# Writing out the two layers of a decoder step, with fewer blocks that clear semaphores

## What is computed

```python
hp, hs = x_prompt, x_sample
for l in range(DEPTH):                       # DEPTH = 2
    mixer_w = (w_in[l], w_conv[l], lower[l], hg_norm[l], w_out[l])
    tail_w = (w_xq[l], w_xo[l], ln2_g[l], ln2_b[l], w_up[l], w_down[l], ln3_g[l], ln3_b[l])
    y, ... = token_mixer(hp, pos_p, *mixer_w, conv0, hg0, dsa_prompt)
    hp = layer_norm(DN_ALPHA * hp + y, ln1_g[l], ln1_b[l])
    hp = cross_and_ffn(hp, mk, mv, *tail_w)
    ...                                      # the same for hs, with paged caches
```

## Time and profile before

| | us |
|---|---|
| median of 3 runs | 3986.69 (3983.5 to 3986.92) |
| the profiled execution | 3984.36 |
| its span, from its first to its last instruction | 3982.5 |

### The profile page before, as it was taken

The page is one execution under the profiler, slowest core; times in us unless marked ns, Lnnn a source line. Parts: engine busy times, 40 slices in busy tenths (PEclk is TensorE's granted clock), DMA queues, the critical chain, the costliest instruction groups (busy, mean ns, idle before and its releaser), DMA issues. The chain is left out here.

```text
span 3982.5 us, 51084 instructions
## 1 busy us (share of the span) xinstructions
PE 3676.5 (92%) x19290; PEld 2740.2 (69%) x19290; DVE 2117.1 (53%) x4222; ACT 1047.1 (26%) x2166; POOL 1176.6 (30%) x1043
## 2 busy tenths in 40 slices
PE   6999978899888999999989999878899889999998
PEld 4454664467677999999845546644666679999997
DVE  4899665553255333333569995555532553333335
ACT  2301133451232221111432112345412321111123
POOL 3014673323032122111430156723120321112224
PEclk9999956999999999999989999579999999999999
DMA  4111002561212111111121010045412121111111
GB/s 150 44 48 39 11 6 91 173 212 53 74 43 85 42 42 42 42 42 42 39 75 43 29 47 6 1 146 178 152 53 74 43 85 42 42 42 42 42 42 56
DMA packets 143260, 255.17 MB, mean 64 GB/s; under 512 B 24801, under 2 KB 76386, under 8 KB 142818
## 3 DMA queue, kind: packets, MB, share of 16 engines
q1 hardware_dynamic: 130786, 215.00, 15.8%
q0 software_dynamic: 12288, 37.76, 2.7%
HBM read 231.31 MB, written 21.42 MB: 63 GB/s over the span
## 5 line engine op out<-in xcount | busy, mean ns | idle before, releaser
L2601 PE MATMUL ps<-ffn_parts 128*128 128x384 f32 (+1 forms) x4608 | 777.2, 329 | 22.7 <-POOL ffn_parts L2766 22.7
L2601 PEld LDWEIGHTS ps<-ffn_parts 128*128 128x128 f32 x4608 | 773.1, 189 | 25.9 <-POOL ffn_parts L2766 23.7
L2611 PE MATMUL ps<-ffn_parts 128*128 128x512 f32 x3328 | 767.9, 390 | 1.9 <-DVE ffn_parts L2823 1.9
L2611 PEld LDWEIGHTS ps<-ffn_parts 128*128 128x128 f32 x3328 | 621.0, 188 | 140.3 <-DVE arena L2836 11.2
L2836 DVE TENSOR_TENSOR arena<-arena,ps 128x1024 f32<-128x1024 f32 x270 | 329.6, 1221 | 304.2 <-PE ps L2611 300.3
L919 PE MATMUL ps<-arena,arena_w 128*128 128x384 f32 (+1 forms) x1152 | 359.5, 475 | 3.6 <-PEq L454 2.6
L2771 POOL TENSOR_TENSOR ffn_parts<-arena,ffn_parts 128x1024 fp32r<-128x1024 f32 x64 | 154.8, 2418 | 566.2 <-ACT ffn_parts L2687 566.2
L928 PE MATMUL ps<-arena_w,arena 128*128 128x512 f32 (+3 forms) x864 | 318.6, 526 | 2.4 <-ACT mix_rest L1104 2.4
L919 PEld LDWEIGHTS ps<-arena,arena_w 128*128 128x128 f32 x1152 | 221.9, 193 | 141.1 <-issue 11.2
L329 DVE TENSOR_SCALAR_CACHE_REDUCE mix_rest<-mix_rest,small 128x384 bf16<-128x384 f32 (+4 forms) x330 | 278.7, 875 | 2.1
L2816 DVE TENSOR_TENSOR arena<-arena 128x384 f32<-128x384 f32 (+1 forms) x96 | 77.0, 829 | 352.7 <-ACT arena L2691 352.7
(11 more groups left out here) (333 smaller groups left out, 5191.7 us busy)
## 6 DMA issues: line engine op xcount, KB each, us to landing
arena<-in_w_down SPq DMA_DIRECT2D x32, 1024.0 KB, 7.4
arena_w<-in_w_in SPq DMA_DIRECT2D x10, 2048.0 KB, 8.5
arena_w<-in_kv SPq DMA_DIRECT2D x64, 256.0 KB
mix_rest<-in_kv SPq DMA_DIRECT2D x64, 256.0 KB
ffn_raw<-in_w_up SPq DMA_DIRECT2D x16, 1024.0 KB, 5.5
arena<-in_w_up SPq DMA_DIRECT2D x16, 1024.0 KB, 5.5
arena<-out_y_prompt SPq DMA_DIRECT2D x2, 4096.0 KB, 14.5
arena_w<-in_mem_kT SPq DMA_DIRECT2D x16, 512.0 KB, 7.0
```

Source lines behind the costliest of these rows:

```text
L2601: ins = pe.matmul(bank(3 * c + b, y - x), w[:, k, :], h[:, k, x:y], start=(k == 0 and h is HH and w is WH), stop=(k == KC - 1 and w is WL))
L2611: ins = pe.matmul(bank((6, 0)[j % 2] + a), u[:, c, tcol(t)] if t < NT - 1 else u[:, c, :], d[:, c, 512 * a:512 * a + 512], start=(first an ...
```

## The change

The loop over the layers becomes a Python loop, so the body stands in the program twice and `layer` is a constant; tensors and semaphores get names with a number. The block that clears ahead of the loop goes. Of the three clears of a layer, the one behind the attention stays a block; the semaphores of the output and cross blocks are cleared by POOL inside `ffn_block`, behind its loop; those of the feed-forward blocks belong to the whole program and are never cleared, each layer having its own. A clear now takes the group's own numbers, one instruction for each run of consecutive numbers. The two stores of x move from the end of the first block to `index_block` of the first layer, behind the loads of `wb` and `par`.

```diff
@@ -128,7 +128,7 @@
         s_kvp = [ctx.enter_context(nc.semaphore(f"kv_gathered{n}")) for n in range(3)]
 
         def sem(name):
-            s = stacks[-1].enter_context(nc.semaphore(name))
+            s = stacks[-1].enter_context(nc.semaphore(f"{name}_{len(groups)}"))
             sems.append(s)
             return s
 
@@ -194,9 +194,6 @@
                              ).then_inc(s_x0, 16)
                 sp.wait_ge(s_c, 32)
                 sp.wait_ge(s_x0, 32)
-                X = at("X", 0, NT, D)
-                sp.dma_start(o["y_prompt"][0].rearrange("(t p) d -> p t d", p=P), X[:, 0:NT - 1, :]).then_inc(s_yo, 16)
-                sp.dma_start(o["y_sample"].rearrange("b t d -> (b t) d"), X[0:NS, NT - 1, :]).then_inc(s_yo, 16)
 
 
             @block.vector
@@ -242,44 +239,52 @@
                 act.wait_ge(chd, 2)
                 act.activation(stat[:, 6:10], stat[:, 6:10], ACT.Exp).then_inc(s_lb, 1)
 
-        def clear_all():
+        def numbers(group):
+
+            nums = sorted(x.num for x in group)
+            cuts = [0] + [k for k in range(1, len(nums)) if nums[k] != nums[k - 1] + 1] + [len(nums)]
+            return [range(nums[a], nums[b - 1] + 1) for a, b in zip(cuts[:-1], cuts[1:])]
+
+        def clear(group):
             with nc.Block() as block:
                 @block.gpsimd
                 def _(pool):
-                    lo = min(s.num for s in sems)
-                    hi = max(s.num for s in sems)
-                    pool.sem_clear(range(lo, hi + 1))
-
-        @contextmanager
-        def own_semaphores():
-
+                    for run in numbers(group):
+                        pool.sem_clear(run)
+
+        def own_semaphores(stack):
+
+            stacks[-1] = stack
+            del sems[:]
+            groups.append(stack)
             env["counts"] = {"dve": 0, "act": 0, "pool": 0}
-            with ExitStack() as part:
-                stacks.append(part)
-                yield
-                clear_all()
-            del stacks[-1]
+            env["chd"], env["cha"], env["chp"] = sem("chain_dve"), sem("chain_act"), sem("chain_pool")
...
-        clear_all()
-        with nc.Fori(0, DEPTH) as layer:
+        for layer in range(DEPTH):
             env["layer"] = layer
-            with nc.sbuf_tensor("arena_w", [P, RR - NHEAD], F32) as rest["w"]:
-                with own_semaphores(), nc.sbuf_tensor("mix_rest", [P, NARENA - RR], F32) as rest["f32"]:
+            with nc.sbuf_tensor(f"arena_w{layer}", [P, RR - NHEAD], F32) as rest["w"]:
+                with ExitStack() as first, nc.sbuf_tensor(f"mix_rest{layer}", [P, NARENA - RR], F32) as rest["f32"]:
+                    own_semaphores(first)
                     index_block(env)
                     mixer_block(env)
                     attend_block(env)
-                with own_semaphores():
-                    with nc.sbuf_tensor("out_parts", [P, OUT_PARTS], F32R) as env["parts"]:
-                        out_block(env)
-                    with (nc.sbuf_tensor("xo_parts", [P, XO_PARTS], F32R) as env["parts"],
-                          nc.sbuf_tensor("cross_rest", [P, NARENA - RR - XO_PARTS], F32) as rest["f32"]):
-                        cross_block(env)
-            with (own_semaphores(), nc.sbuf_tensor("ffn_raw", [P, FFN_RAW], F32) as rest["w"],
-                  nc.sbuf_tensor("ffn_parts", [P, FFN_PARTS], F32R) as env["parts"]):
+                    clear(sems)
+                second = ExitStack()
+                own_semaphores(second)
+                with nc.sbuf_tensor(f"out_parts{layer}", [P, OUT_PARTS], F32R) as env["parts"]:
+                    out_block(env)
+                with (nc.sbuf_tensor(f"xo_parts{layer}", [P, XO_PARTS], F32R) as env["parts"],
+                      nc.sbuf_tensor(f"cross_rest{layer}", [P, NARENA - RR - XO_PARTS], F32) as rest["f32"]):
+                    cross_block(env)
+            env["done_with"] = numbers(sems)
+            own_semaphores(ctx)
+            with (nc.sbuf_tensor(f"ffn_raw{layer}", [P, FFN_RAW], F32) as rest["w"],
+                  nc.sbuf_tensor(f"ffn_parts{layer}", [P, FFN_PARTS], F32R) as env["parts"]):
                 ffn_block(env)
+            second.close()
 
 
         with nc.Block() as block:
@@ -457,6 +462,9 @@
             sp.dma_start(wb, lay(i["w_in"], layer).rearrange("l (k p) n -> p (l k) n", p=P)[:, :, A_QI:NIN]
                          ).then_inc(s_w, 16)
             sp.dma_start(e["par"][:, :], lay(i["params"], layer).rearrange("l p n -> (l p) n")).then_inc(s_par, 16)
+            if layer == 0:
+                sp.dma_start(o["y_prompt"][0].rearrange("(t p) d -> p t d", p=P), X[:, 0:NT - 1, :]).then_inc(e["s_yo"], 16)
+                sp.dma_start(o["y_sample"].rearrange("b t d -> (b t) d"), X[0:NS, NT - 1, :]).then_inc(e["s_yo"], 16)
 
             sp.wait_ge(s_ro, NT)
             sp.dma_start(lay(o["kidx_prompt"], layer).rearrange("l b (t p) d -> p (l b t) d", p=P),
@@ -2781,6 +2789,8 @@
             with pool.Fori(0, G2) as g2:
                 for n in range(2):
                     group_weights(g2, n)
+            for run in e["done_with"]:
+                pool.sem_clear(run)
             group_weights(G2, 0)
             for c in range(FFC):
                 for half in range(2):
```

More of the change, by code:

```diff
@@ L18 @@
-from contextlib import ExitStack, contextmanager
+from contextlib import ExitStack
 import concourse.bass as bass
@@ L122, in build @@
         ps = ctx.enter_context(nc.psum_tensor("ps", [P, 8 * 512], F32))
-        sems, stacks, rest = [], [ctx], {}
+        sems, stacks, groups, rest = [], [ctx], [], {}
         s_kit = ctx.enter_context(nc.semaphore("cached_kidx"))
```

## The result

The changed kernel takes 3961.78 us, the median of 4 executions (3956.68, 3958.13, 3965.43 and 3967.78). Beside them the kernel before took 3985.1 (4 executions, 3982.47 to 3986.92). The ratio is 0.9943, with a 95% interval of 0.9925 to 0.9961: faster, by 23 us in the median.

The account below looks back on a forecast made before the run. TensorE, busy 3676.5 of 3982.5 us, bounds the kernel, so only its standstills can be won. 9.4 (start) + 2.2 (clears) + 4.7 (between layers) = 16.3 us; from halfway between two bases, 3969 us, range 3964 to 3977.

Parts of the forecast that it names:

- The start, up to the first transpose: Before TensorE's first transpose: the first block ends earlier, so the transpose comes at 25.2 us, 1.9 us earlier (bounds 1.7 and 2.0).
- The index weights: First layer's index block: weights issued ahead of the stores end a 5.96 us wait, and 1.5 us for slower products behind it.
- The stores and the relu: First index block: moved stores land at 44.3 us, before ACT's first relu needs them at about 50.6; cover 6.3 us.
- rival 3: First index block: moved stores hold up ACT's relus and the scores; slower, 3995.4 us if they land at 77; chance 0.03.
- The clears: Ahead of the feed-forward block 1.1 us saved, twice, 2.2; the remaining clear unchanged (bounds -0.5 and +0.5); those inside cost nothing.
- rival 4: Inside the feed-forward block: seventeen or more clear runs exceed POOL's 13.72 us pause; 3970 us and up; chance 0.02.
- Between the layers: From layer 0's end to layer 1's first transpose: clear block and TensorE's branch back go, 4.7 us gained, 0.1 left.
- Rival 2: Between the layers: TensorE's stop stays because new code is not there yet; 3.3 us back, 3972.3 us; chance 0.08.
- The end: Kernel's end: last clear block and loop exit go, but the landing of out_y_prompt sets the end, so nothing gained.
- Rival 1: First index block: stores served alongside the weights, which land near 44; 7.5 us lost, 3976.5 us; chance 0.10.
- How the numbers follow: The prediction's chances: 0.72 for 3964 to 3974 us, 0.88 for faster, under 3978.7; 0.09 within 0.2%, 0.03 slower.
- rival 5: Whole kernel: lower-clock stretches fall differently, 1.7 us per group of products; five more would give 3977.5 us; chance 0.05.

## Why the prediction was right in its steps and wrong in its range

- *The start, up to the first transpose*: 1.9 us was right as a length but did not show in the profile. From SP's last wait to the first transpose it took 26.1 to 26.61 instead of 24.7 to 27.10; x itself landed 1.4 us later in this execution, so 0.5 is left of it there. In the three profiles of the changed kernel the first transpose starts anywhere from 25.36 to 26.61.
- *The index weights*: the mechanism was right, and the term was too small. I took 5.96 + 1.5 us from one profile. The index block from first transpose to release takes 120.23, 122.24 and 121.43 us in the kernel before, with the stores back, and with the layers written out alone; it takes 111.90, 111.86 and 112.6 in three profiles of the changed kernel. That is 121.3 - 112.1 = 9.2 us instead of 7.5. The profile of before had the smallest of these waits (5.96 us, 6.40 in the other two), and the clock adds to it in places that differ: with the layers written out alone the group after the wait took 6.91 us instead of 5.74; with the stores back it took 5.56, but the eighth index product took 5.94 instead of 4.25, which is the 1.7 us that the prediction took at nothing.
- *The stores and the relu*: expected 44.3 and 50.6, seen 45.6 with the sample rows (44.6 for the large store) and 51.4. The cover of some 6 us was there; rival 3 did not happen.
- *The clears*: 0.1 us was expected from release to first cast, and it is there. The clear that stays went from 0.90 to 1.20 us: 0.3 us for each layer lost, just outside the bounds given (0.5 for both). In layer 1 the trace has three runs there (0.29, 0.15 and 0.18 us); in layer 0 it has a single record of 0.55 us, so what took the time there isn't shown. The clears inside the feed-forward block cost nothing; rival 4 did not happen.
- *Between the layers*: 4.7 us expected, 4.85 to 0.1 seen. Rival 2 fell with the kernel that has the layers written out alone. The Trainium skill, Runtime: NRT & Kernel Launch, section Instruction fetch mechanics, says that fetching runs ahead sequentially and that a taken branch out of the pages held forces a fetch. The traces agree: five instruction packets at the jump, none where the code is in line.
- *The end*: nothing was expected; the two blocks' ends go, and SP's wait for the last store grows from 0.6 to 1.9 us. Right:

```profile
SPq L290 <- DMA out_y_prompt<-arena: 1.9, 1, 1.9
```

- *Rival 1* fell: the weights landed 6.4 us after their issue although the stores were issued 1.1 us behind them.

With the corrected terms the sum is 16.3 + 1.7 - 0.6 = 17.4 us, inside the 18.4 ± 2.7 of all executions. The step that failed is in "How the numbers follow": "2 us either way from the bases". I took the scatter from three executions within 3.4 us. The kernel before scatters from 3975 to 3997 over 59 executions and the changed one from 3957 to 3976 over 15, so a median of four lies some us from the long-run value without any cause in the edits. Over all 15 it is 3966.0, inside the range. From 3969 down to 3961.78 it is 7.2 us: 1.4 because the base, halfway between 3984.36 and 3986.69, lay above the 3984.1 of 59 executions; 1.1 for the terms; the other 4.7 are where four executions happened to fall. I had seen one piece of the reason, but put rival 5, the clock, at 0.05 and only upward.

In one stage the traces show the clock at work by itself. The first output block takes 157.92 us in the first profile of the changed kernel and 155.06 in the third, from release to release. The products are the same, and TensorE waits alike, 6.09 us at the start and 2.8 near the end; behind these waits it runs slower in the first (upper two rows):

```profile
858.80 35.49 PE L2060 MATMUL ps<-out_parts 128*128 128x512 f32 x144 [6.09 <-DVE out_parts L2171]
998.62 11.58 PE L2099 MATMUL ps<-arena,arena_w 128*128 128x384 f32 x32
...
858.80 34.31 PE L2060 MATMUL ps<-out_parts 128*128 128x512 f32 x144 [6.09 <-DVE out_parts L2171]
996.84 10.49 PE L2099 MATMUL ps<-arena,arena_w 128*128 128x384 f32 x32
```

Over the 5 us behind the second wait the granted clock was 0.66 in the first and 1.00 in the third. The profiled execution of the kernel with 9 idle products is the only one under 3960 us with a trace: 3956.43, 11.35 less than the changed kernel's. There the second index block is 3.0 us shorter, the two output blocks 2.9 and 3.0, and the first cross-attention block 2.4, all three at a clock 0.01 to 0.02 higher.

That the clock goes with the time is shown by the executions; that it alone makes the scatter is not: waits for DMA, as for in_kv and for x, differ as well. Why two of the first four executions came out at 3957 and 3958 stays open, since neither has a trace.

## What to carry to other kernels

Look at the order of a queue at the head of each stage: a store that nothing waits for soon, put ahead of the load that the next stage waits for, cost 9 to 11 us in the first index block here, for two lines moved. A pause costs twice where TensorE falls to the lower clock in it, so price a wait together with the first products behind it. And before giving a range for an effect of half a per cent, get the scatter from more than three executions: the sum came within some 2 us of the mean of all executions, the median of four did not.

## What the runs showed of the hardware that was not expected

- TensorE's granted clock behind the border of the layers depended on what it did in the pause before. After a pause of 10.19 us at the border of the layers the second index block ran at a mean of 0.97 and took 112.95 us; with idle products up to 2.45 us ahead of it, it ran at 1.00 and took 109.93 (109.74 and 109.94 in the two other kernels with them). At the start of the kernel the same means did not hold the clock.
- The full clock too early can cost: with 8 idle products ahead of the feed-forward block TensorE ran ahead of its inputs, paused for 3.23 us instead of 0.90, and the block took 790.30 us instead of 788.50.
- One jump back over a whole layer cost TensorE 3.3 us, with five packets on the instruction queues beside it, while the same code in line cost 0.1.
